# A relative-position bias table that is read back in order from 32 DRAM copies, without flip products

## What is computed

```python
def t5_bucket(n):                      # n = t - s >= 0
    n = jnp.maximum(n, 0)
    max_exact = N_BUCKETS // 2
    nf = jnp.maximum(n, 1).astype(jnp.float32)
    large = max_exact + (jnp.log(nf / max_exact) / math.log(MAX_DISTANCE / max_exact)
                         * (N_BUCKETS - max_exact)).astype(jnp.int32)
    large = jnp.minimum(large, N_BUCKETS - 1)
    return jnp.where(n < max_exact, n, large)
...
        bias = jnp.swapaxes(rel_bias[t5_bucket(dist)], -1, -2)
        logits = (jnp.einsum('bthd,btkhd->bthk', qb, kg).astype(jnp.float32) * (D ** -0.5)
                  + bias.astype(jnp.float32))
```

## Time and profile before

| | value |
|---|---|
| median of three executions | 1134.96 us (1133.47 to 1135.14) |
| the profiled execution, its own time | 1133.52 us |
| its span, first to last instruction | 1132.2 us |
| TensorE (PE) busy | 1119.0 us, 99% |
| VectorE (DVE) busy | 822.3 us, 73% |
| ScalarE (ACT) busy | 637.5 us, 56% |
| transfers | 231.10 MB, mean 204 GB/s |
| granted TensorE clock | 0.999 |

### The profile page before, as it was taken

One profiled execution on the slowest core, in us unless ns is written; L12 is line 12 of the kernel. 1 busy time (PEld: TensorE's weight loads), 2 busy tenths in 40 slices (PEclk: granted clock), 3 DMA queues, 4 the chain that ended last, 5 costly groups with the idle time before them and its releaser, 6 DMA issues.

```text
span 1132.2 us, 16844 instructions
## 1 busy us (share of the span) xinstructions
PE 1119.0 (99%) x6542; PEld 980.1 (87%) x6542; DVE 822.3 (73%) x1416; ACT 637.5 (56%) x1203; POOL 56.8 (5%) x68
## 2 busy tenths in 40 slices
PE   8999999999999999999999999999999999999997
PEld 6998989799988888888899988888889988888886
DVE  6988878798666766676777867666667866766665
ACT  6664444856757755555755556544556654555553
POOL 2200000000001000000012300000001100000000
PEclk9999999999999999999999999999999999999999
DMA  9989999594232766668453326555554434655530
GB/s 385 419 317 380 321 368 263 226 344 154 104 113 75 243 212 221 221 223 208 145 187 112 117 108 224 186 189 186 190 182 166 167 112 149 213 189 192 191 128 37
DMA packets 36992, 231.10 MB, mean 204 GB/s; under 512 B 6825, under 2 KB 8241, under 8 KB 9522
## 3 DMA queue, kind: packets, MB, share of 16 engines
q1 hardware_dynamic: 31536, 225.59, 56.7%
q10 hardware_dynamic: 5378, 4.45, 1.3%
HBM read 228.95 MB, written 1.07 MB: 203 GB/s over the span
## 4 chain that ended last, share of the span: by engine, by line
PE 86%; DVE 5%; ACT 5%; DMA 2%; issue 1%; POOL 1%; ACTq 0%; DVEq 0%; POOLq 0%
PE ps L1722 43%; PE pacc L1722 42%; DVE wlo L2274 1%; ACT whi L2002 1%; DMA raw<-in_stream 1%; ACT arena L2109 1%; ACT wk L2212 1%; DMA cl<-in_cols 1%; POOL st L2604 1%; DVE st L2499 0%; PE ps L1861 0%; DVE wk L2493 0%; DVE wlo L2284 0%; PE ps L1932 0%; DVE h L2390 0%
## 5 line engine op out<-in xcount | busy, mean ns | idle before, releaser
L2274 DVE TENSOR_TENSOR wlo<-raw,whi 128x1024 fp32r<-128x1024 f32 x346 | 414.9, 1223 | 115.3 <-ACT whi L2002 115.1
L1722 PE MATMUL ps<-both,whi 128*128 128x256 f32 (+2 forms) x1728 | 460.7, 339 | 1.4 <-DVE both L2365 0.6
L2002 ACT ACTIVATE whi<-raw 128x1024 fp32r<-128x1024 f32 x346 | 360.4, 1056 | 100.6 <-PE ps L1722 46.5
L1722 PE MATMUL ps<-both,wlo 128*128 128x256 f32 x1264 | 354.6, 281 | 0.0
L1722 PEld LDWEIGHTS ps<-both,whi 128*128 128x128 f32 (+1 forms) x1728 | 296.9, 189 | 41.9 <-issue 3.1
L1722 PEld LDWEIGHTS ps<-both,wlo 128*128 128x128 f32 x1264 | 238.8, 189 | 2.9
L1722 PE MATMUL pacc<-whi,both 128*128 128x512 f32 (+2 forms) x352 | 106.4, 383 | 1.0 <-ACT both L2125 0.6
L2002 ACT ACTIVATE sg<-ps 128x256 f32<-128x256 f32 (+1 forms) x98 | 37.3, 380 | 100.2 <-PE ps L1722 100.2
L2294 DVE SCALAR_TENSOR_TENSOR raw<-raw,silu_c 128x1024 f32<-128x1024 f32 x72 | 89.9, 1256 | 1.8 <-DMA raw<-in_stream 1.6
L1722 PE MATMUL pacc<-whi,mhi 128*128 128x512 f32 x228 | 90.7, 398 | 0.0
L1722 PE MATMUL pacc<-whi,mlo 128*128 128x512 f32 x228 | 89.5, 392 | 0.0
(11 more groups left out here) (280 smaller groups left out, 1471.9 us busy)
## 6 DMA issues: line engine op xcount, KB each, us to landing
raw<-in_stream SPq DMA_DIRECT2D x213, 1024.0 KB, 5.0
gates<-gate_rows ACTq DMA_DIRECT2D x3, 512.0 KB, 6.6
h<-in_x SPq DMA_DIRECT2D x2, 512.0 KB, 4.2
cst<-in_const ACTq DMA_DIRECT2D x1, 1024.0 KB, 4.7
arena<-bias_rows ACTq DMA_DIRECT2D x1, 1024.0 KB, 25.9
arena<-in_final_g SPq DMA_DIRECT2D x1, 512.0 KB, 5.8
out<-tmp SPq DMA_DIRECT2D x2, 256.0 KB, 2.0
out<-tmp ACTq DMA_DIRECT2D x2, 256.0 KB, 2.3
```

Source lines behind the costliest of these rows:

```text
L1722: return e.matmul(o, a, b, start=start, stop=stop)
L2002: return e.activation(o, a, ACT.Copy, **how)
L2274: return e.tensor_tensor(o, a, hi.bitcast(F32), ALU.subtract)
```

## The change

The rows are stored 32 times in DRAM (`bias_rows` becomes 32 x 8 x 384), by one DMA whose source repeats each of the 8 rows in `wk` 32 times. They are read back with a partition pitch of 3072 - 1 elements, so that each next partition begins in the next copy but one element earlier: the windows land in the wanted order, directly in `table`. One DMA covers 32 partitions, so there are four. The flip matrix, `staged`, the four products and their four copies are gone. `sparse` waits for the four DMAs instead of the last copy.

```diff
-for _name, _n in (..., ("strict", 128), ("flip", 128),
+for _name, _n in (..., ("strict", 128),
...
         add("table_back")
-        for _ in range(12):
-            yield
-        for n in range(4):
-            b = banks.take()
-            add("table_flip", n=n, b=b.at, free=b.free, full=tick("tab"))
-            got["table"] = tick("tabc")
-            banks.give(b, got["table"])
-            yield
+        got["table"] = ("table_in", 64)
...
-        self.scratch = nc.dram_tensor("bias_rows", [8, 384], F32).ap()
+        self.scratch = nc.dram_tensor("bias_rows", [32, 8, 384], F32).ap()
...
-        self.table, self.staged = self.arena[:, 10496:12544], self.arena[:, 6144:8192]
+        self.table = self.arena[:, 10496:12544]
...
-        elif kind == "table_flip":
-            q.wait_ge("table_in", 16)
-            q.room(st.free)
-            mul(m.bank(st.b), m.const("flip"), m.staged[:, half(st.n)], True, True).then_inc(S["tab"], 1)
...
             q.wait_ge("tabc", 1)
-            e.dma_start(m.scratch, m.wk[0:8, 6, :]).then_inc(S["rows_out"], 16)
+            e.dma_start(m.scratch.rearrange("b h x -> h b x"), m.wk[0:8, 6:7, :].to_broadcast([8, 32, 384])).then_inc(S["rows_out"], 16)
         elif kind == "table_back":
             q.wait_ge("rows_out", 16)
-            e.dma_start(m.staged.rearrange("p (h s) -> p h s", h=8), bass.AP(
-                tensor=m.scratch.tensor, offset=0, ap=[[1, P], [384, 8], [1, T]])).then_inc(S["table_in"], 16)
-        elif kind == "table_flip":
-            q.wait_ge(*st.full)
-            copy(m.table[:, half(st.n)], m.bank(st.b)).then_inc(S["tabc"], 1)
+            for a in range(0, P, 32):
+                rows = bass.AP(tensor=m.scratch.tensor, offset=127 - a, ap=[[8 * 384 - 1, 32], [384, 8], [1, T]])
+                e.dma_start(m.table[a:a + 32, :].rearrange("p (h s) -> p h s", h=8), rows).then_inc(S["table_in"], 16)
```

More of the change, by code:

```diff
@@ L46 @@
 _at = 0
-for _name, _n in (("ident", 128), ("ones", 128), ("rot", 128), ("tri", 128), ("causal", 128), ("strict", 128), ("flip", 128),
+for _name, _n in (("ident", 128), ("ones", 128), ("rot", 128), ("tri", 128), ("causal", 128), ("strict", 128),
                   ("cos", 256), ("sin", 256), ("topk", 512), ("bucket", 384)):
@@ L2659, in constants @@
     put("rot", r)
-    put("flip", np.eye(P)[::-1])
     put("tri", (i[:, None] >= i[None, :]).astype(np.float32))
```

## The result

The change makes the kernel slower, by 1.0%. Its median is 1145.76 us (1142.06 to 1149.82, six runs) against 1133.67 us (1133.43 to 1135.14, six runs) of the kernel before: ratio 1.0102, 95% interval 1.0082 to 1.0123. The forecast was 1133.7 us and at most 1137.5, a change of -1.2 us counted from a median of 1134.96; measured are +12.1 us. The profiled execution is the quickest of the six, 1142.06 us with a span of 1140.7, so it explains 8.5 us of span; the 3.7 us between it and the median have no profile.

The account below looks back on a forecast made before the run. TensorE, busy 99% of the span, was taken to bound the kernel. Flips -3.43, stall +1.7 and later idle time +0.5 gave -1.2 us: from 1134.96 to 1133.7 us, 8-in-10 range 1130.8 to 1137.5 us.

Parts of the forecast that it names:

- What goes: Flips at 138 to 153 us: removing their TensorE passes saves 3.43 us; removing their ScalarE copies saves nothing.
- What hides for nothing: Read-back landing, shorter constants and other PSUM banks cost nothing; the table is first used at 302.4 us.
- What is added: ScalarE waits for the larger store, 12.75 us, plus three more issues: 1.7 us of idle TensorE near 107 us.
- the half-engine pace: Store's upper estimate: only half of the DMA engines share it, its source lying in 8 partitions; 15.4 us to land.
- the rule quoted in the prediction: Outermost dimension under 16 confines a DMA to that many engines; here 8 heads, so 15.4 us for the store.
- What is late next: After the stall, through gate_out's thin stretch: time won back and lost nearly cancel, 0.5 us of idle TensorE.
- The 3 us won back in 20: After the stall, VectorE's splits were to win back at most some 3 us in the next 20 us.
- VectorE's 15%: VectorE is busy 10.16 of 12 us at 110 to 122 us, so it can win back at most 15%.
- (C): ScalarE's wait for the store in table_back makes the kernel slower, from a landing at 102.3 us on: 1138.4 us; chance 0.17.
- (B): The forecast itself: part of the flips' gain goes into idle TensorE, -1.2 us, 1133.7 us; chance 0.40.
- (A): Store lands inside the cover, by 99.2 us, so the whole 3.43 us stay: 1131.5 us; chance 0.36.
- (D): No saving: the weight stream, not TensorE, sets the pace between 124 and 150 us: 1135.0 us; chance 0.07.

Follow-up runs that it names:

- e2: Kernel before without its four flips, one read straight into the table, small store kept: 1131.42 us, ratio 0.9980.
- e9: The change with store from 128 partitions, read-backs to every fourth partition, and the wait and read-backs 16 yields after the store: 1130.43 us, ratio 0.9967.
- e3: Kernel before with only the 384 KB store from 8 partitions put in, flips and one read-back kept: 1138.42 us, ratio 1.0040.
- e12: Kernel before with the 384 KB store, from 128 partitions, flips and one read-back kept: 1135.00 us, ratio 1.0012.
- e10: The change with only the wait and read-backs moved, to 16 yields after the store instead of one: 1135.16 us, ratio 1.0008.
- e11: The change with store from 128 partitions and the wait and read-backs 16 yields after the store: 1131.26 us, ratio 0.9978.
- e4: The change with gate_out stored as 128 runs of 32 bytes instead of 1024 single numbers: 1135.90 us, ratio 1.0016.
- e1: The change with the wait and read-backs four yields after the store instead of one: 1147.89 us, ratio 1.0124.
- e7: The change with the store from 128 partitions, two copies each, instead of from 8: 1138.97 us, ratio 1.0039.
- e8: The change with store from 128 partitions and read-backs to every fourth partition, wait not moved: 1139.52 us, ratio 1.0052.

## Why the prediction was wrong

**What goes: right.** No flip products, 3.43 us forecast; e2 shows 3.6 in the spans and 2.5 in the medians, e9 3.3.

**What hides for nothing: wrong in one point.** `sparse` isn't late, as said. But I looked only at the landing of the read-backs, and not at what they take from the stream meanwhile: 0.61 MB of chunks at 102 to 110 us where the kernel before moved 2.83 MB.

**What is added: right in kind and nearly in size.** The store took 11.4 us (forecast 12.75), the four issues 2.39 (forecast 1.65), and the first idle time of PE is 1.0 us, before 109 (forecast 1.7, near 107). The upper bound for the store went by the half-engine pace, 15.4 us; it named 5.8 us as the lower end, but took the middle of 10.1 and 15.4. The read's 25.9 us, from which both come, is no fixed pace: the same read took 16.3 us in e3 and 7.0 in e12. In "DMA: Bandwidth & Descriptors", Rules for kernel authors, the Trainium skill has the rule quoted in the prediction; the pair e3 and e12, 218 against 422 GB/s beside the same bytes, agrees with it in direction. I used it for the store's own landing. Its larger effect was on the neighbour: e10 and e11, which never stand, are 3.9 us apart by it. The prediction's own sign of being wrong, "if the store itself slows the stream so much that chunks, not ACT, are late", had named this.

**What is late next: this is the step that failed.** It said "Won back and lost nearly cancel: I take 0.5 us of idle PE (0 to 2.5)". Measured are 2.4 us of idle PE and 1.7 us of lost clock at 130 to 140, then 3.6 us and 2.7 us at 203 to 214: 10.4 us in place of 0.5. Four things went wrong in it. The 3 us won back in 20 need a full stream, and the stream had 76 GB/s at 102 to 110, held by the reads. VectorE's 15% holds for 110 to 122 us and not later: the chain ahead of the third gap, at 149 to 182 us, has it working nearly without a pause, and four hidden blocks take it 32.8 us, against 34.1 for PE, so it wins back 1.3 us in 33 and not 3 in 20. The 2.5 us that `gate_out`'s thin stretch costs were taken from a kernel that met it with 8.7 us of spare, and had 6.2 left behind it; here the rings came to it with less than its 8 us at 116 GB/s took. And the sum ended at 155 us with "not reshaped", though VectorE's chain shows no ring filled again until the second `gate_out` at 191.7, whose gap cost more than the first one's. e4 shows the chain of cause for the second gap: thin stretch taken away, stand left, the gap gone, and 9.9 of 12.1 us in all. e10 shows it from the other end: stand taken away and reads moved, thin stretches left, 10.6 us gone. Neither alone is the cause; it takes the empty rings and the thin stretch together. For the third gap that is half shown: e4 keeps 3.2 us of it with no thin stretch, on VectorE's pace, and e10 3.4 us with no stand.

**The clock.** The prediction had each us of late weights as one us. After idle times of 2.4 and 3.6 us the granted clock fell to 0.50, and 4.4 us more went there. It isn't a fixed price: after e4's 3.2 us it stayed at 1.00.

**The rivals.** (C) named the right place and sign, and the landing was 99.8, below its deciding point of 102.3 us (its own sum, 99.2 + 3.43, gives 102.6); what decided was the second and third collision, which it priced at 2.5. (B) gave its range in two ways: 2.2 us around -1.2 is 1131.6 to 1136.0, not 1132.7 to 1136.5; neither range holds the result. (A) would need a landing 0.6 us earlier; but in e3 the store is there at 98.43, inside its cover, PE has no idle time near 107, and 4.5 us are lost all the same, and e4, with the reads issued at 98.69, no idle PE near 107 and no first thin stretch either, is still above the kernel before. (D) is out by e2 and e9.

**Still open.** Why the runs of the change scatter over 7.8 us and those of e9 mostly over 1. Whether `gate_out` in e1 landed so late because of the reads ahead of it. By what mechanism 32 neighbouring partitions slow a neighbour's transfer: only that the place of the destination does it is shown. How much of the third gap is VectorE's pace and how much the thin stretch. Why the clock fell behind two gaps and not behind e4's. How the loss of each gap divides between clock and waiting is worked out from windows, not isolated by a run.

## What to carry to other kernels

Before an in-order engine is made to wait, ask how much spare its ring has and also whether the ring gets that spare back before the next thin stretch of the stream; if it doesn't, the later thin stretches reach the last engine, and its clock may fall behind each gap. A DMA of few bytes is to be judged by what it does to the others: here 384 KB from 8 partitions left the stream 1.29 MB in 6 us, and from 128 partitions 2.42 MB (e10 and e11), and four reads into 32 neighbouring partitions each left it 3.66 MB in 12 us, into every fourth partition 4.28 MB (e11 and e9, 158 to 170 us). A result that isn't needed for 200 us is fetched late, behind the last wait that it could disturb.

## What the runs showed of the hardware

- A store of 384 KB from 8 partitions: 208 to 271 GB/s in all beside it (92 to 98 us, seven runs), landing in 10.3 to 12.7 us. From 128 partitions: 401 to 422 GB/s, 6.8 to 9.7 us.
- Four reads of 256 KB behind a stand: 9.1 us to landing into 32 neighbouring partitions each, 4.6 us into every fourth one; beside a full stream 19.7 (e11) and 13.3 us (e9). With one read of 1 MB into all 128 partitions the rate was 393 GB/s; that read took 7.0 to 27.4 us.
- 1024 single numbers written to DRAM: 116 GB/s at 122 to 130 us; with 128 runs of 32 bytes the same stretch had 418 GB/s.
- Four DMA issues in a row on ScalarE took 0.34, 0.46, 0.51 and 0.98 us in the change, none over 0.48 in e7, and 3.06 us together in e8, where one alone takes 0.41.
- After 2.4 us without a product the granted clock (1 is 2.4 GHz) was 0.71, 0.50 and 0.94 in the next windows of 2 us, after 3.6 us 0.50, 0.50 and 0.66, and after e4's 3.2 us 1.00.
